# Another order around the first two weight groups, in the last two halves of a decoder layer's mixing weights

## The reference

```
h = x + 0.5 * swiglu(rms_norm(x, ffn1_norm), ...)
z = rms_norm(h, mix_norm) @ w_in + b_in            # q, k, v of both mixers, two gates
ya = dilated_attention(...)                        # mixer A: 12 heads in 3 groups of 4
yb = sliding_window_sink_attention(...)            # mixer B: 8 heads, window 128, sinks
merged = sigmoid(ga) * (ya @ w_branch_a) + sigmoid(gb) * (yb @ w_branch_b)
h = h + merged @ w_out
h = h + 0.5 * swiglu(rms_norm(h, ffn2_norm), ...)
return rms_norm(h, final_norm)
```

```
alpha = jax.nn.softmax(jnp.stack(lses, axis=0), axis=0)
y = jnp.sum(alpha[..., None] * jnp.stack(outs, axis=0).astype(jnp.float32), axis=0)
```

## Time and profile before

| | |
|---|---|
| median of 3 runs | 2070.58 us (2070.49 to 2071.46) |
| the profiled execution | 2070.9 us |
| its span | 2069.1 us |
| mean granted clock of TensorE | 0.994 of full speed |
| TensorE busy | 2034.4 us, 98% |
| VectorE busy | 1397.6 us, 68% |
| ScalarE busy | 793.4 us, 38% |
| GpSimd busy | 159.4 us, 8% |

### The profile page before, as it was taken

One profiled execution on the slowest core, in us unless ns is written; L12 is line 12 of the kernel. 1 busy time (PEld: TensorE's weight loads), 2 busy tenths in 40 slices (PEclk: granted clock), 3 DMA queues, 4 the chain that ended last, 5 costly groups with the idle time before them and its releaser, 6 DMA issues.

```text
span 2069.1 us, 26547 instructions
## 1 busy us (share of the span) xinstructions
PE 2034.4 (98%) x9442; PEld 1654.8 (80%) x9442; DVE 1397.6 (68%) x2333; ACT 793.4 (38%) x1493; POOL 159.4 (8%) x144
## 2 busy tenths in 40 slices
PE   8999999999999999999998999999999999999998
PEld 6878888888888777777776888887878888888886
DVE  7976666666987454566775443458876676666976
ACT  6343233334455243443545112134333333334453
POOL 1000000000022000142440000012000000000011
PEclk9999999999999999999999999999999999999998
DMA  5233233266436011001114111123233233266433
GB/s 183 77 117 112 82 117 107 77 219 247 150 125 206 31 41 42 31 31 42 45 48 148 46 51 51 51 77 122 77 123 107 90 112 110 77 226 247 137 102 117
DMA packets 85804, 217.41 MB, mean 105 GB/s; under 512 B 9195, under 2 KB 9231, under 8 KB 83888
## 3 DMA queue, kind: packets, MB, share of 16 engines
q1 hardware_dynamic: 69568, 164.66, 23.2%
q10 hardware_dynamic: 14480, 46.16, 6.3%
q0 software_dynamic: 1632, 4.98, 0.7%
HBM read 160.68 MB, written 55.08 MB: 104 GB/s over the span
## 4 chain that ended last, share of the span: by engine, by line
PE 89%; DVE 5%; issue 3%; ACT 1%; DMA 1%; POOL 0%; POOLq 0%; ACTq 0%; DVEq 0%; SPq 0%
PE bank L1965 20%; PE bank L1967 20%; PE bank L1966 20%; PE bank L1911 9%; PE bank L1913 8%; PE bank L1912 8%; PE bank L2154 1%; PE bank L2117 1%; PE bank L2130 1%; PE bank L2186 1%; DVE op_l L1368 0%; PE bank L2167 0%; DMA z_in<-gz 0%; DVE wl L1290 0%; DVE sp L1735 0%
## 5 line engine op out<-in xcount | busy, mean ns | idle before, releaser
L1911 PE MATMUL bank<-xh,wh 128*128 128x512 f32 x640 | 256.7, 401 | 0.0
L1965 PE MATMUL bank<-B_h,op_h 128*128 128x512 f32 x624 | 245.8, 394 | 8.2 <-DVE op_l L1368 8.0
L1965 PE MATMUL bank<-T_h,op_h 128*128 128x512 f32 x640 | 249.3, 390 | 1.9 <-DVE U L1459 1.9
L1912 PE MATMUL bank<-xl,wh 128*128 128x512 f32 x640 | 249.9, 391 | 0.0
L1913 PE MATMUL bank<-xh,wl 128*128 128x512 f32 x640 | 249.9, 390 | 0.0
L1966 PE MATMUL bank<-T_l,op_h 128*128 128x512 f32 x640 | 249.0, 389 | 0.0
L1967 PE MATMUL bank<-T_h,op_l 128*128 128x512 f32 x640 | 249.0, 389 | 0.0
L1967 PE MATMUL bank<-B_h,op_l 128*128 128x512 f32 x624 | 243.8, 391 | 0.0
L1966 PE MATMUL bank<-B_l,op_h 128*128 128x512 f32 x624 | 243.8, 391 | 0.0
L1965 PE MATMUL bank<-gs_h,op_h 128*128 128x512 f32 x616 | 240.5, 390 | 0.7 <-DVE gs_l L1402 0.7
L1967 PE MATMUL bank<-gs_h,op_l 128*128 128x512 f32 x616 | 239.7, 389 | 0.0
(11 more groups left out here) (211 smaller groups left out, 3503.4 us busy)
## 6 DMA issues: line engine op xcount, KB each, us to landing
gr<-g_ops SPq DMA_DIRECT2D x154, 256.0 KB, 2.7
raw<-stream SPq DMA_DIRECT2D x56, 512.0 KB, 3.5
gate<-ffn_in SPq DMA_DIRECT2D x44, 512.0 KB, 4.0
up<-ffn_in SPq DMA_DIRECT2D x44, 512.0 KB, 4.9
g_ops<-tT SPq DMA_DIRECT2D x78, 256.0 KB, 2.0
g_ops<-gb SPq DMA_DIRECT2D x58, 256.0 KB, 5.0
A<-ffn_down ACTq DMA_DIRECT2D x6, 1536.0 KB, 7.8
h_spill<-h ACTq DMA_DIRECT2D x32, 256.0 KB, 2.3
```

Of the source, the lines that this page charges most:

```text
L1911: nc.tensor.matmul(out, wh[slot][:, cols], hi, start=first, stop=False)
L1912: nc.tensor.matmul(out, wh[slot][:, cols], lo, start=False, stop=False)
L1965: nc.tensor.matmul(out, op_h[slot][:, cols], hi, start=first, stop=False, skip_group_check=True)
```

## The change

In the steps with `start` 2 and 3 the events around the first two groups of mixing weights change places. In step 27 the first two groups no longer stand around the transposes; both stand behind the value product. In step 31 the value product moves ahead of the transposes, right behind the first group. No event is added, removed or altered.

```diff
+            early_pv = start == 3
-            if misc:
+            if misc and start != 2:
                 plan.append(misc.pop(0))
+            if early_pv:
+                plan.append(("pv", c - PV_LAG))
             if 0 <= c - T_LAG < CHUNKS:
                 plan.append(("t", c - T_LAG))
             if 0 <= c - 1 < CHUNKS:
                 plan.append(("den", c - 1))
-            if misc:
+            if misc and start != 2:
                 plan.append(misc.pop(0))
-            if 0 <= c - PV_LAG < CHUNKS:
+            if 0 <= c - PV_LAG < CHUNKS and not early_pv:
                 plan.append(("pv", c - PV_LAG))
+            if start == 2:
+                plan += [misc.pop(0), misc.pop(0)]
             if misc and start is None:
                 plan.append(misc.pop(0))
```

## The result

| | before | changed |
|---|---|---|
| median | 2070.59 us (2069.64 to 2072.09, 20 runs) | 2073.53 us (2071.14 to 2075.06, 20 runs) |
| ratio to before, 95% interval | | 1.0014 [1.0008, 1.0021] |
| the profiled execution | 2070.9 us | 2073.55 us |
| its span | 2069.1 us | 2071.7 us |

The account below looks back on a forecast made before the run. TensorE, busy 98% of the span, was taken as the bound. 4.4 us lost at chunk 27 less 1.5 gained at chunk 31 made 2.9 slower: 2073.5 us, own range 2072 to 2074.6, full range 2070.2 to 2075.6.

Parts of the forecast that it names:

- T25 and V24 start early: Chunk 27: transposes run from 995.2, value product ends at 997.1; TensorE's wait shrinks from 1.76 to about 0.8 us.
- Copy G0 stands behind den26, scale26 and the subtraction: Chunk 27: VectorE's copy of the first weight group starts about 1001.5 and ends at 1002.2, instead of starting at 997.11.
- G1 waits for it: Chunk 27: the second weight group waits for the copy of bank 7; TensorE idles 4.5 us, projection queued behind.
- the rival by which G1 doesn't wait: Chunk 27's second weight group needs no copy: 2.2 us gained there, 5.0 faster in all, 2065.6 us; chance 0.04.
- The clock at the first place: Chunk 27: half clock until 1006.6 after the wait, so the projection loses 1.7 us.
- The sum of the first place: Chunk 27: projection ends at 1010.5 instead of 1006.04, 4.4 us lost; bounds 2.3 and 5.6.
- The second place: Chunk 31: value product and transposes fill the wait for the copy; 1.5 us gained, bounds 0.7 and 2.8.
- the first: Rival: the clock stays down longer, 5.6 us lost at chunk 27, 0.7 gained at chunk 31, 2075.5 us; chance 0.20.
- the second: Rival: the clock hardly matters, 2.3 us lost at chunk 27, 2.8 gained at chunk 31, 2070.1 us; chance 0.09.
- the third: Rival: TensorE's 4.5 us wait for z_in at the first merging step absorbs the slip, 2070.6 us; chance 0.09.
- The rule weighed: Skill page advises against TensorE gaps over about 3 us; by it chunk 31 gains 2.8 us and the sum is 1.6 slower.

Follow-up runs that it names:

- late_copy: Kernel before, TensorE's order untouched, VectorE's copy of the first weight group at chunk 27 moved behind the scaling of chunk 26; 2076.0 us, ratio 1.0027.
- bank0: Changed kernel, with the second weight group of chunk 27 written to bank 0 instead of bank 7; 2065.86 us, ratio 0.9978.
- before_again: Kernel before, unedited, profiled once more; 2070.2 us in one execution.
- again: Changed kernel, unedited, profiled once more; 2070.56 us in one execution.
- only_first: Kernel before with the new order at chunk 27 alone; 2075.13 us, ratio 1.0023.
- bank0_first: Changed kernel with chunk 27's second weight group in bank 0 and the old order at chunk 31; 2068.62 us, ratio 0.9989.
- only_second: Kernel before with the new order at chunk 31 alone; 2069.34 us, ratio 0.9995; timed once more, 2069.71 us, ratio 0.9996.
- between: Changed kernel with chunk 27's first weight group between the transposes and the value product, both groups in bank 7; 2068.2 us, ratio 0.9987.

## Why the prediction was right, step by step

- *T25 and V24 start early.* T25 at 995.2 predicted, 995.12 measured, V24 ended at 997.0; PE's first wait is 0.87 (about 0.8).
- *Copy G0 stands behind den26, scale26 and the subtraction.* Predicted to start at 1001.5, it started at 1001.04. Den26 came 0.2 earlier, and scale26 took 1.22 us instead of 1.53: before, GpSimd built operands beside it (the last section has the other traces).
- *G1 waits for it.* 4.5 predicted, 4.20 measured, and shown as the cause: `late_copy` has the loss by the copy alone, `bank0` takes the wait away and has no loss. This also settles the rival by which G1 doesn't wait, though its price (2065.6) is what `bank0` measured (2065.9). That G1 "never waited" for this copy in the old order holds for the first profile alone: where the clock stayed full, as in `before_again`, it waited 0.60 us.
- *The clock at the first place.* Full at 1006.6 predicted, and the stretches show half to 1006 and full from 1007. A projection of 7.40 us loses 1.83 (1.7 predicted). The sum of the first place, 4.4, came out as 4.07. In `again` and `only_first` the clock came back sooner, and the projection took 6.6; yet before's own first profile was the longer of its two as well (12.75 against 11.95), so the two orders differ by 4.1 where the longer is set beside the longer or the shorter beside the shorter (16.82 - 12.75, 16.04 - 11.95), and by 3.3 to 4.9 crosswise. `only_first` timed 4.7.
- *The second place: here the term was mis-sized.* 1.5 us predicted, with 2.8 as a bound; the first pair of profiles shows 3.0 (14.45 to 11.46). I took T29, V28 and G1 at half clock, 4.23 us, because the old order's wait of 2.15 had been followed by half clock. That was the exception: in the other four traces of the old order T29 ran at full clock (1.09) behind this wait, and the clock fell only in the second one. In five of seven executions of the new order the clock stayed up behind a wait of 2.5, and in none of five of the old order, whose two waits together come to some 3.1 to 3.7 us. The wait for copy G0 that the change covers was also larger than I read it: 0.94 us in the one trace, because T29 ran at half clock there, and 1.60 in `before_again`, `only_first`, `bank0_first` and `late_copy`. What this is worth in the time of the whole kernel is less sure: the medians give 1.6 (changed against `only_first`), 1.1, 0.9 and 2.8 us, three of the four nearer to the 1.5 predicted than to 3.0.
- *What the prediction did not have.* The fall of the clock after chunk 36, 1.6 us. In the first pair of profiles it cancelled the 1.5 that the second place gained beyond its term, so that there the sum came near 2.9 (2.6 by the spans) with two errors that made up for each other. That is luck. The second pair, `again` against `before_again`, has 4.1 lost, 3.5 gained and no such fall, and its spans are only 0.4 us apart. The median of 2.9 over 20 runs is thus not accounted for by the two places alone; what else the clock did in those runs stays open. The fall after chunk 36 was seen in three of seven profiles with the new order at the second place and in none of five with the old, which is too little to call it a consequence of the change. It may be why the second place by itself shows 3 us in a profile and only 1.1 and 0.9 us in two sets of timings, while `bank0` against `bank0_first` gives it 2.8. That was not settled: where the clock fell is known for twelve executions only. Of the others the mean granted clock is known. In `only_second` it was 0.996 in the two fastest (2067.76 and 2068.16 us) and 0.993 or 0.994 in the three slowest (2070.15 to 2071.81), so a lower clock goes with the longer times.
- *The rivals.* The clock came back sooner than in the first (the first place lost 4.07, not 5.6); it mattered, against the second (1.83 us of the first place are clock); the wait for z_in is still 4.5 us, as before, against the third.

- *The rule weighed.* The first profile of before had half clock after 1.76 us, and `before_again` had it after waits of 2.14 and 1.60, so gaps under 3 us can cost the clock. The gap of 4.2 us was followed by half clock in all three traces that have it. At the second place, though, five of seven executions kept it behind 2.5 us. By the Trainium skill's page (TensorE: Matmul & The Clock Gate, "Why this matters for your kernels") that place would gain 2.8 us, which is near what the place itself shows in most traces. Neither the rule nor what I set against it, that a wait of that size costs the clock each time, holds for all executions.

## What to carry to other kernels

Where several engines walk through one shared list, moving an event moves its half on each engine. The question is not only what the producer waits for, but what stands ahead of the reader in the reader's queue: an engine that waits for something else can't reach a copy that would free a bank. If the order is wanted for other reasons, give the next writer another bank, or move the reader past that wait; both turned a loss of 2.9 us into a gain (`bank0` 4.6, `between` 2.3). And where a change shortens or joins waits on TensorE, take more than one profile before sizing the clock's share.

## What the runs showed of the hardware

- The same wait was followed by either clock. After 1.76 us for GpSimd's operand, the stretch was at 0.50 in the first profile of before, and in `before_again` it was

```profile
996.80:998.40 1.60, 1.00 (x9) 0.76 (x8) 1.38 (x3) 1.60 (x7) 1.34 (x3) 1.00 0.00 0
```

- In the changed kernel's first profile the clock fell behind waits of 0.84 and 0.80 us, with no other wait in the eight us ahead of them; in nine of the twelve traces it stayed full behind the same two:

```profile
1092.00:1096.00 4.00, 4.00 (x26) 3.00 (x26) 3.02 (x15) 2.61 (x10) 0.00 (x0) 0.59 0.01 4
```

- VectorE's scaling of 128x1024 at the first place took 1.53 us beside GpSimd's operand builds in the kernel before, and 1.38 or 1.39 in seven other traces, where the builds overlap only its start. It took 1.22 or 1.23 with GpSimd idle, in the changed kernel, `again`, `only_first` and `late_copy`. The last two builds took 2.16 us beside it in the kernel before and 1.18 or 1.19 in `before_again` and `between`, so both took longer side by side.
